# Moving three small products from inside a TensorE group to the boundary one half group earlier

## The chip, the cores and the metric

The kernel runs on one core of one Trainium2 chip. The time is device microseconds of one execution. A core has five engines with queues of their own: TensorE (PE, with its weight loads shown apart as PEld), VectorE (DVE), ScalarE (ACT), GpSimd (POOL) and SyncE (SP). Each takes its instructions in the order in which they are written and waits at a semaphore until another engine or a DMA has counted it up. Everything here is written by hand in that form: one list of instructions for each engine, and named semaphores between them.

## The reference, cut to what matters

Two transformer blocks of width 1024 over 1024 tokens, in fp32. The first ends with a feed-forward layer; the second is scaled and shifted by a vector `mod` that hangs on the input `c` alone:

```
# end of the first block
hid = square(relu(einsum("bsd,df->bsf", h, w_mlp_in)))      # 1024 -> 4096
x   = x + einsum("bsf,fd->bsd", hid, w_mlp_out)             # 4096 -> 1024
# start of the second block
c_act = silu(c)                                             # (1, 1024)
mod   = c_act @ w_ada + b_ada                               # (1, 6144)
sh1, sc1, gt1, sh2, sc2, gt2 = split(mod, 6)
```

`mod` is needed only once the first block is done. The kernel computes it during the first block's feed-forward layer, and that is the place of the change.

## The kernel before, in words

A product of two fp32 matrices is made from three products of high and low parts (hi·hi, lo·hi, hi·lo), all summed in one PSUM bank. A **group** is one 128x512 tile of a result: `group(g, b, ...)` waits on the semaphore `group_free` until bank `b` is empty, issues all matmuls of the tile through `product`, and counts `group_done`.

The feed-forward layer (`ff`) goes through the 4096 hidden columns in eight chunks of 512. Each chunk `i` has on TensorE:
- eight **up groups** n = 0 to 7 of 24 matmuls (8 pieces of the contraction, 3 products each): they fill banks 0 to 3 in turn. ACT takes each result through relu, square and a copy to the high part (lines 864, 866, 870), DVE makes the low part (`hid_lo`, line 1435) and so frees the bank.
- sixteen **down groups** of 12 matmuls (t = 0 to 7, m = 0, 1), which DVE adds to the residual (`xs`, line 1479) and so frees the bank.

Weights come by DMA from SP through four buffers `w_raw`, ACT makes their high part (`w_hi`, line 646) and DVE their low part (`w_lo`, line 1056).

`mod` is made in the six middle chunks (i = 1 to 6) of the first block's layer, 1024 columns of it in each chunk, in four quarters of 256. For one quarter (index n = 0 to 3 of `modulation` on PE) DVE adds up eight **rows**, r = 8n to 8n + 7, into the tile `ada_sum` (line 1452 for the first, line 1454 for the other seven); each row is 128x256 of `w_ada`, weighted by a column of silu(c). Two rows come with one DMA, issued from POOL (line 567), into one of two buffers; POOL issues a DMA when the rows of the one before last are used up. Then PE sums `ada_sum` over the partitions: two matmuls with `one` as the moving operand, of one column each, into bank 4 (line 2048; the profile counts each in two passes, so four). On PE they stand behind a wait for the eight rows. The semaphore `ada_mm` tells DVE that `ada_sum` may be written again, and the first row of the next quarter waits for it.

On DVE the rows stand behind the low parts of the up groups: four behind each of groups 0 to 5, and eight behind group 6. Before the low part of group 0 stand the eight low parts of the weights for the down groups, and behind that of group 7 those for the next up groups, and then the first `xs`. So quarter 0 is complete after the rows behind up group 1, quarter 1 after those behind group 3, quarter 2 after those behind group 5, and quarter 3 after those behind group 6.

On PE the sums of quarters 0, 1 and 2 stand in the middle of up groups 3, 5 and 7, between its twelfth and thirteenth matmul (`between`, lines 1736 and 2062). The sum of quarter 3 stands behind the second down group.

Of the kernel before, what the change touches and what calls it, by code (L numbers as in the profile page):

```python
# [6 lines left out]
def build(nc, a, out):  # L7
# [7 lines left out]
    P = 128  # L15
# [29 lines left out]
    with ctx:  # L45
# [18 lines left out]
        def act_pair(name, o):  # L64
            return (at(name + "_hi", [P, 8, HALF], f32r, o), at(name + "_lo", [P, 8, HALF], f32r, o + SLOT // 2))
# [110 lines left out]
        h2 = [act_pair("h2_0", s2), act_pair("h2_1", s3)]  # L176
# [40 lines left out]
        bank = [ctx.enter_context(nc.psum_tensor(f"bank{i}", [P, 512], f32)) for i in range(8)]  # L217
        XB = bank[4:]

        def sem(name):  # L220
            return ctx.enter_context(nc.semaphore(name))
# [3 lines left out]
        group_done, group_free = sem("group_done"), sem("group_free")  # L225
# [1502 lines left out]
        def _(pe):  # L1728
            mm = nc.tensor.matmul

            def product(out, pairs, between=None):

                n = len(pairs)
                for i, ((lh, ll), (rh, rl)) in enumerate(pairs):
                    if between and i == n // 2:
                        between()
                    mm(out, lh, rh, start=(i == 0), stop=False)  # L1737
                    mm(out, lh, rl, start=False, stop=False)  # L1738
                    last = mm(out, ll, rh, start=False, stop=(i == n - 1))  # L1739
                return last  # L1740

            def group(g, b, width, pairs, rows=P, between=None):
                if not (isinstance(g, int) and g < 4):
                    pe.wait_ge(group_free, g - 3)
                product(bank[b][0:rows, 0:width], pairs, between).then_inc(group_done, 1)

            def chunk_ready(c):
                pe.wait_ge(w_lo, 8 * (c + 1))
# [25 lines left out]
            for j in range(2):  # L1774
                group(j, j, MEM, [((w[0][:, k, j * P:(j + 1) * P], w[1][:, k, j * P:(j + 1) * P]),
                                   (memT[0][:, k, :], memT[1][:, k, :])) for k in range(8)])
            for j in range(2):
                group(2 + j, 2 + j, MEM, [((memT[0][:, k, j * P:(j + 1) * P], memT[1][:, k, j * P:(j + 1) * P]),
                                           (w[0][:, k, 256:512], w[1][:, k, 256:512])) for k in range(8)])
# [5 lines left out]
            def natural(c, par, g, t, width):  # L1785
                group(g, g % 4, width, [(tok(hT, k, t), (W[par][0][:, k, 0:width], W[par][1][:, k, 0:width]))
                                        for k in range(8)])
# [143 lines left out]
            for u, (b, h) in enumerate(ISC):  # L1931
                n = (b + 1) * P
# [14 lines left out]
            with pe.Fori(1, 3) as i:  # L1947
                for j in range(2):
                    par = (C_GATE + j) % 2
                    chunk_ready(2 * i + (C_GATE + j))  # L1950
                    for n in range(8):
                        f, h = n // 2, n % 2
# [72 lines left out]
            for c in range(2):  # L2025
                par = (C_OUT + c) % 2
                chunk_ready(C_OUT + c)
                for t in range(NT):
                    if c == 0 and t % 4 == 0:
                        pe.wait_ge(st_lo, 8 * (t // 4 + 1))  # L2030
                    g = GO + 8 * c + t
                    group(g, g % 4, 512, [(tok(mT, k, t), (W[par][0][:, k, :], W[par][1][:, k, :])) for k in range(8)])

            def norm_transposes(n0, x0, h):
                transposes(n0 + 8 * h, [[xn[:, 4 * h + j, k * P:(k + 1) * P] for j in range(4)] for k in range(8)],
                           lambda n: (n_xn, x0 + 4 * (h + 1)) if n == 0 else None)
                pe.wait_ge(n_lo, n0 + 8 * h + 8)

            def ff(c0, g0, k, n0, x0):


                pa, pb = c0 % 2, 1 - c0 % 2

                def modulation(i, n):

                    pe.wait_ge(ada_s, i * 32 + (8 * n + 8 - 32))
                    for e in range(2):
                        l = mm(bank[4][:, ds(i * 8 + (2 * n + e - 8), 1)], adac[:, e * P:(e + 1) * P], one[:, :],
                               start=True, stop=True)
                    l.then_inc(ada_mm, 1)  # L2050

                def chunk(i, first, last):
                    mod = not (k or first or last)
                    chunk_ready(2 * i + c0)
                    for n in range(8):
                        h, f = n // 4, n % 4
                        if first and n == 4:
                            norm_transposes(n0, x0, 1)
                        group(i * 24 + (g0 + n), n % 4, 512,
                              [((W[pa][0][:, q, f * P:(f + 1) * P], W[pa][1][:, q, f * P:(f + 1) * P]),  # L2060
                                (h2[h][0][:, q, :], h2[h][1][:, q, :])) for q in range(8)],
                              between=(lambda: modulation(i, (n - 3) // 2)) if mod and n in (3, 5, 7) else None)
                    chunk_ready(2 * i + (c0 + 1))
                    for t in range(NT):
                        h, q = t // 4, (t % 4) * P
                        if t % 4 == 0:
                            pe.wait_ge(f_lo, i * 8 + (8 * FC * k + 4 * (h + 1)))
                        for m in range(2):
                            group(i * 24 + (g0 + 8 + 2 * t + m), (2 * t + m) % 4, 512,
                                  [((hid[h][0][:, f, q:q + P], hid[h][1][:, f, q:q + P]),  # L2070
                                    (W[pb][0][:, 2 * f + m, :], W[pb][1][:, 2 * f + m, :])) for f in range(4)])
                            if mod and t == 0 and m == 1:
                                modulation(i, 3)

                norm_transposes(n0, x0, 0)
                if not k:
                    pe.sem_inc(ada_mm, 1)
                chunk(0, True, False)
                with pe.Fori(1, FC - 1) as i:
                    chunk(i, False, False)  # L2080
                chunk(FC - 1, False, True)

            ff(C_FF, GF, 0, 24, 10)
# [27 lines left out]
            for n in range(4):  # L2111
                q = slice((n % 2) * 256, (n % 2) * 256 + 256)
# [38 lines left out]
            for g in range(4):  # L2151
                for par, c in ((0, C_U), (1, C_K)):
                    if g == 0:
                        chunk_ready(c)
                    for h in range(2):
                        n = 2 * par + h
# [102 lines left out]
```

## Time and profile before

| what | us |
|---|---|
| median of 3 runs | 2933.64 |
| lowest and highest of them | 2927.18, 2936.40 |
| the profiled execution, by its own time | 2927.18 |
| its span | 2925.1 |
| the six chunks with `mod` (about) | 1020 to 1560 of the span |

TensorE is busy for 92% of the span, DVE for 48%, ACT for 34% and POOL for 12%. Start times in all rows are microseconds from the start of the span. The six chunks follow each other at 91.4 to 93.5 us, so that what is read in the first stands five more times behind it.

### The profile page before, as it was taken

What the parts mean: (1) busy time and instruction counts of PE and PEld (TensorE: products, weight loads), DVE (VectorE), ACT (ScalarE), POOL (GpSimd) and SP (SyncE); (2) the same over time, 40 slices, a digit from 0 to 9 for tenths busy, and PEclk for the clock granted to TensorE, in tenths of its full rate; (3) what the DMA queues carried; (4) which work ended last, traced back from release to release, by engine and by line L of the source; (5) the groups of instructions that cost most, each with busy time, mean ns of one, the idle gap of its engine ahead of it and who ended that gap; (6) DMA issues with size and microseconds to landing.
All of it is one profiled execution on the core that took longest, in us unless ns stands there. A gap on an engine that the chain in (4) does not pass through costs nothing.

```text
span 2925.1 us, 35932 instructions
## 1 busy us (share of the span) xinstructions
PE 2677.9 (92%) x12620; PEld 2183.2 (75%) x12620; DVE 1417.3 (48%) x3008; ACT 1005.6 (34%) x2052; POOL 339.8 (12%) x524
## 2 busy tenths in 40 slices
PE   5996899988989999999999899977788999999997
PEld 4764788865767788887888677767677888888886
DVE  5266479855543344444543533228444345434345
ACT  6156267545123223221322442236134222223222
POOL 0222512230320011001110000014000000000000
PEclk9999999999999999999999899999799999999998
DMA  4002123331530133222321122131411111011011
GB/s 161 26 30 72 50 76 98 101 129 59 185 122 11 58 116 103 77 90 75 115 90 54 44 84 87 44 101 44 166 36 58 34 53 57 30 56 57 29 43 65
DMA packets 110981, 218.21 MB, mean 75 GB/s; under 512 B 12412, under 2 KB 24324, under 8 KB 110612
## 3 DMA queue, kind: packets, MB, share of 16 engines
q1 hardware_dynamic: 90836, 164.29, 17.2%
q0 software_dynamic: 11968, 37.77, 4.2%
q10 hardware_dynamic: 8064, 14.68, 1.3%
q8 instruction: 66, 1.08, 0.2%
q14 instruction: 47, 0.39, 0.0%
HBM read 183.07 MB, written 33.63 MB: 74 GB/s over the span
## 4 chain that ended last, share of the span: by engine, by line
PE 78%; DVE 9%; ACT 5%; DMA 4%; issue 3%; POOL 1%; SPq 0%; DVEq 0%; ACTq 0%; POOLq 0%
PE bank L1737 23%; PE bank L1739 22%; PE bank L1738 22%; DVE w_lo L1056 1%; ACT w_hi L646 1%; PE bank L1914 1%; PE bank L1915 1%; PE bank L1916 1%; PE bank L1834 1%; DMA w_raw<-in_w_mlp_in 1%; DMA ada<-in_w_ada 1%; DMA w_raw<-in_w_ff 1%; ACT bank L903 1%; ACT h_hi L906 1%; PE bank L1823 1%
## 5 line engine op out<-in xcount | busy, mean ns | idle before, releaser
L1737 PE MATMUL bank<-h_hi,w_hi 128*128 128x512 f32 (+1 forms) x1312 | 516.1, 393 | 19.2 <-DVE h_lo L1522 8.4
L646 ACT ACTIVATE w_hi<-w_raw 128x512 fp32r<-128x512 f32 (+3 forms) x440 | 257.1, 617 | 766.4 <-PE bank L1739 565.0
L1738 PE MATMUL bank<-h_lo,w_hi 128*128 128x512 f32 (+1 forms) x1312 | 511.6, 390 | 0.0
L1739 PE MATMUL bank<-h_hi,w_lo 128*128 128x512 f32 (+1 forms) x1312 | 511.5, 390 | 0.0
L1737 PE MATMUL bank<-w_hi,hid_hi 128*128 128x512 f32 x1024 | 402.2, 393 | 19.5 <-DVEq L1481 19.4
L1739 PE MATMUL bank<-w_hi,hid_lo 128*128 128x512 f32 x1024 | 399.8, 390 | 0.0
L1738 PE MATMUL bank<-w_lo,hid_hi 128*128 128x512 f32 x1024 | 399.5, 390 | 0.0
L1056 DVE TENSOR_TENSOR w_lo<-w_raw,w_hi 128x512 fp32r<-128x512 f32 (+3 forms) x384 | 253.8, 697 | 210.2 <-ACT w_hi L646 203.8
L1737 PEld LDWEIGHTS bank<-h_hi,w_hi 128*128 128x128 f32 x1312 | 249.5, 190 | 73.7 <-DVE h_lo L1522 9.0
L1739 PEld LDWEIGHTS bank<-h_hi,w_lo 128*128 128x128 f32 x1312 | 249.2, 190 | 51.6
L1738 PEld LDWEIGHTS bank<-h_lo,w_hi 128*128 128x128 f32 x1312 | 249.4, 190 | 50.8 <-issue 0.7
L1435 DVE TENSOR_TENSOR hid_lo<-bank,hid_hi 128x512 fp32r<-128x512 f32 x128 | 88.6, 692 | 390.1 <-ACT hid_hi L870 388.6
L1479 DVE TENSOR_TENSOR xs<-xs,bank 128x512 f32<-128x512 f32 x256 | 175.9, 687 | 185.3 <-PE bank L1739 173.8
L1737 PEld LDWEIGHTS bank<-w_hi,hid_hi 128*128 128x128 f32 x1024 | 193.0, 189 | 65.3 <-DVEq L1481 25.8
L1739 PEld LDWEIGHTS bank<-w_hi,hid_lo 128*128 128x128 f32 x1024 | 192.8, 188 | 40.6
L1738 PEld LDWEIGHTS bank<-w_lo,hid_hi 128*128 128x128 f32 x1024 | 193.2, 189 | 39.5
L864 ACT ACTIVATE bank<-bank 128x512 f32<-128x512 f32 x128 | 74.5, 582 | 383.8 <-PE bank L1739 383.8
L567 POOL DMA_DIRECT2D ada<-in_w_ada x96 | 69.5, 724 | 633.4 <-DVE ada_sum L1454 633.2
L1477 DVE TENSOR_TENSOR bank<-bank,rowv 128x512 f32<-128x512 f32 x128 | 89.5, 699 | 104.9 <-PE bank L1739 92.1
L1258 DVE TENSOR_SCALAR_CACHE_REDUCE cmpj<-isc,cand 128x384 bf16<-128x384 f32 (+1 forms) x124 | 100.5, 811 | 7.4 <-DVE cand L1269 5.0
L1454 DVE SCALAR_TENSOR_TENSOR ada_sum<-ada,cact,ada_sum 128x256 f32<-128x256 f32 x168 | 81.5, 485 | 41.4 <-DMA ada<-in_w_ada 34.1
L533 POOL TENSOR_TENSOR w_lo<-w_raw,w_hi 128x512 fp32r<-128x512 f32 x56 | 74.9, 1347 | 227.4 <-ACT w_hi L646 223.0
(401 smaller groups left out, 4138.1 us busy)
## 6 DMA issues: line engine op xcount, KB each, us to landing
w_raw<-in_w_ff SPq DMA_DIRECT2D x128, 256.0 KB, 3.1
w_raw<-in_w_in SPq DMA_DIRECT2D x104, 256.0 KB, 2.7
ada<-in_w_ada POOLq DMA_DIRECT2D x96, 256.0 KB, 3.2
w_raw<-in_w_mlp_in SPq DMA_DIRECT2D x64, 256.0 KB, 3.2
w_raw<-in_w_mlp_out SPq DMA_DIRECT2D x64, 256.0 KB, 3.0
gates_scratch<-gstage ACTq DMA_DIRECT2D x32, 256.0 KB, 2.0
w_raw<-in_w_out SPq DMA_DIRECT2D x32, 256.0 KB, 4.5
stage<-gates_scratch SPq DMA_DIRECT2D x8, 768.0 KB, 5.1
```

The source lines that it names most:

```text
L533: nc.gpsimd.tensor_tensor(W[par][1][:, p, :], raw[:, p % NRAW, :], W[par][0][:, p, :].bitcast(f32), ALU.subtract).then_inc(w_lo, 1)
L646: A_(W[par][0][:, p, 0:n], raw[:, p % NRAW, 0:n], ACT.Copy).then_inc(w_hi, 1)
L864: A_(x, x, ACT.Relu).then_inc(f_r, 1)
L1056: tt(W[par][1][:, p, 0:n], raw[:, p % NRAW, 0:n], W[par][0][:, p, 0:n].bitcast(f32), ALU.subtract).then_inc(w_lo, 1)
L1258: tsc(cmpj[:, 0:(b + 1) * P], isc[b][:, :], cand[:, b - 2:b - 1].bitcast(f32), None, ALU.is_ge, ALU.add, accum_out=cnt[:, b - 2:b - 1]).th ...
L1435: tt(hid[h][1][:, f, :], bank[n % 4][:, :], hid[h][0][:, f, :].bitcast(f32), ALU.subtract)\
L1454: l = stt(adac[:, :], x, cact[:, k:k + 1], adac[:, :], ALU.mult, ALU.add)
L1477: tt(b, b, rowv[:, 512 * m:512 * m + 512], ALU.mult).then_inc(gt_x, 1)
L1479: tt(x, x, bank[(2 * t + m) % 4][:, :], ALU.add).then_inc(x_add, 1)
L1737: mm(out, lh, rh, start=(i == 0), stop=False)
L1738: mm(out, lh, rl, start=False, stop=False)
L1739: last = mm(out, ll, rh, start=False, stop=(i == n - 1))
```

## The change

`product` and `group` lose their parameter `between`. The sums of quarters 0, 1 and 2 now stand behind up groups 2, 4 and 6, that is ahead of all 24 matmuls of groups 3, 5 and 7 instead of behind the first twelve. Quarter 3 stays where it is. The other engines' instructions are the same and in the same order.

```
-            def product(out, pairs, between=None):
+            def product(out, pairs):
 
                 n = len(pairs)
                 for i, ((lh, ll), (rh, rl)) in enumerate(pairs):
-                    if between and i == n // 2:
-                        between()
                     mm(out, lh, rh, start=(i == 0), stop=False)
...
                         group(i * 24 + (g0 + n), n % 4, 512,
                               [((W[pa][0][:, q, f * P:(f + 1) * P], W[pa][1][:, q, f * P:(f + 1) * P]),
-                                (h2[h][0][:, q, :], h2[h][1][:, q, :])) for q in range(8)],
-                              between=(lambda: modulation(i, (n - 3) // 2)) if mod and n in (3, 5, 7) else None)
+                                (h2[h][0][:, q, :], h2[h][1][:, q, :])) for q in range(8)])
+                        if mod and n in (2, 4, 6):
+                            modulation(i, (n - 2) // 2)
```

Here is TensorE's queue at the sum of quarter 0 before the change, in the middle of up group 3. `ada_sum` is DVE's sum of the rows, `h_0` the layer's input, and the row in which the wait stands is the weight load of the sum.

```order
L1737 MATMUL bank<-h_0_hi,w_hi 128x512
L1738 MATMUL bank<-h_0_lo,w_hi 128x512
L1739 MATMUL bank<-h_0_hi,w_lo 128x512
L2046 ISA
L2048 ISA [waits ada_sum]
L2048 MATMUL bank<-one,ada_sum 128x1
L2048 ISA
L2048 MATMUL bank<-one,ada_sum 128x1
L1737 MATMUL bank<-h_0_hi,w_hi 128x512
L1738 MATMUL bank<-h_0_lo,w_hi 128x512
```

And here is the same queue after it, at the boundary of up groups 2 and 3 (its line numbers are two lower).

```order
L1735 MATMUL bank<-h_0_hi,w_hi 128x512
L1736 MATMUL bank<-h_0_lo,w_hi 128x512
L1737 MATMUL bank<-h_0_hi,w_lo 128x512
L2044 ISA
L2046 ISA [waits ada_sum]
L2046 MATMUL bank<-one,ada_sum 128x1
L2046 ISA
L2046 MATMUL bank<-one,ada_sum 128x1
L1742 REGISTER_ALU
L1735 MATMUL bank<-h_0_hi,w_hi 128x512 [waits group_free]
```

The wait for the rows has moved ahead of the twelve matmuls that stood between the start of group 3 and the sum, and with it stands ahead of the whole of group 3. Quarters 1 and 2 move in the same way.

## Rows read from the trace of the kernel before

**Rows 1.** The page: busy us of each engine, share of the span, instructions.

```profile
PE 2677.9 (92%) x12620; PEld 2183.2 (75%) x12620; DVE 1417.3 (48%) x3008; ACT 1005.6 (34%) x2052; POOL 339.8 (12%) x524
```

**Rows 2.** Who waited for whom, 1020 to 1560: total us, times, longest.

```profile
PE bank L1737 <- DVEq L1481: 13.3, 6, 2.7
```

**Rows 3.** Timeline, PE, first chunk, group 3: start, us, instruction, [idle before <-releaser].

```profile
1037.52 0.39 PE L1737 MATMUL bank<-h_hi,w_hi 128*128 128x512 f32 x1
...
1040.01 0.64 PEld L2048 LDWEIGHTS bank<-one,ada_sum 128*128 128x128 f32 x4
1040.24 0.50 PE L2048 MATMUL bank<-one,ada_sum 128*128 128x1 f32 x4
...
1040.60 0.48 PE L1737 MATMUL bank<-h_hi,w_hi 128*128 128x512 f32 x1
```

**Rows 4.** Timeline, ACT's relu: ends of groups 2, 3, 4; group 2, chunks 3, 4.

```profile
1037.72 0.58 ACT L864 ACTIVATE bank<-bank 128x512 f32<-128x512 f32 x1 [3.61 <-PE bank L1739]
...
1043.65 0.58 ACT L864 ACTIVATE bank<-bank 128x512 f32<-128x512 f32 x1 [4.11 <-PE bank L1739]
...
1049.09 0.58 ACT L864 ACTIVATE bank<-bank 128x512 f32<-128x512 f32 x1 [3.61 <-PE bank L1739]
...
1222.20 0.58 ACT L864 ACTIVATE bank<-bank 128x512 f32<-128x512 f32 x1 [3.61 <-PE bank L1739]
...
1313.65 0.58 ACT L864 ACTIVATE bank<-bank 128x512 f32<-128x512 f32 x1 [3.61 <-PE bank L1739]
```

**Rows 5.** Timeline, DVE: last rows of quarter 0, chunks 1, 3, 4.

```profile
1038.22 1.00 DVE L1454 SCALAR_TENSOR_TENSOR ada_sum<-ada,cact,ada_sum 128x256 f32<-128x256 f32 x2 [0.39 <-DMA ada<-in_w_ada]
...
1222.89 1.01 DVE L1454 SCALAR_TENSOR_TENSOR ada_sum<-ada,cact,ada_sum 128x256 f32<-128x256 f32 x2 [0.58 <-DMA ada<-in_w_ada]
...
1313.89 1.01 DVE L1454 SCALAR_TENSOR_TENSOR ada_sum<-ada,cact,ada_sum 128x256 f32<-128x256 f32 x2 [0.39 <-DMA ada<-in_w_ada]
```

**Rows 6.** Timeline: quarters 1 and 2, last rows on DVE and sums on PE.

```profile
1057.79 2.05 DVE L1454 SCALAR_TENSOR_TENSOR ada_sum<-ada,cact,ada_sum 128x256 f32<-128x256 f32 x4 [0.21 <-DVE hid_lo L1435]
...
1062.99 0.50 PE L2048 MATMUL bank<-one,ada_sum 128*128 128x1 f32 x4
...
1139.09 1.01 DVE L1454 SCALAR_TENSOR_TENSOR ada_sum<-ada,cact,ada_sum 128x256 f32<-128x256 f32 x2 [0.23 <-DMA ada<-in_w_ada]
...
1143.04 0.50 PE L2048 MATMUL bank<-one,ada_sum 128*128 128x1 f32 x4
```

**Rows 7.** The chain of waits, second chunk: start, us, what.

```profile
1154.57 0.35 PE bank L2048 x4
...
1155.03 0.36 DVE ada_sum L1452
...
1157.25 3.53 DMA ada<-in_w_ada
...
1162.00 0.70 DVE hid_lo L1435
...
1165.00 3.54 DMA w_raw<-in_w_mlp_in
```

**Rows 8.** Timeline, DVE behind low parts 0 and 6; PE's release, first chunk.

```profile
1032.45 0.35 DVE L1452 TENSOR_SCALAR ada_sum<-ada,cact 128x256 f32<-128x256 f32 x1 [0.33 <-DVE hid_lo L1435]
...
1062.32 0.69 DVE L1435 TENSOR_TENSOR hid_lo<-bank,hid_hi 128x512 fp32r<-128x512 f32 x1 [2.49 <-ACT hid_hi L870]
1063.60 0.36 DVE L1452 TENSOR_SCALAR ada_sum<-ada,cact 128x256 f32<-128x256 f32 x1 [0.59 <-DMA ada<-in_w_ada]
...
1079.06 0.68 DVE L1479 TENSOR_TENSOR xs<-xs,bank 128x512 f32<-128x512 f32 x1
...
1079.85 0.50 PE L1737 MATMUL bank<-w_hi,hid_hi 128*128 128x512 f32 x1 [2.12 <-DVEq L1481]
```

**Rows 9.** Stretches of 1 us: busy us (x) by engine, granted clock, DMA share, GB/s.

```profile
1172.00:1173.00 1.00, 1.00 (x4) 0.81 (x3) 0.70 (x2) 0.00 (x0) 0.00 (x0) 0.50 0.79 262
...
1357.00:1358.00 1.00, 1.00 (x4) 0.81 (x3) 0.70 (x2) 0.00 (x0) 0.00 (x0) 0.50 0.72 240
```

More of the change, by code:

```diff
@@ L1740, in product, with group @@
                 return last
-            def group(g, b, width, pairs, rows=P, between=None):
+            def group(g, b, width, pairs, rows=P):
                 if not (isinstance(g, int) and g < 4):
                     pe.wait_ge(group_free, g - 3)
-                product(bank[b][0:rows, 0:width], pairs, between).then_inc(group_done, 1)
+                product(bank[b][0:rows, 0:width], pairs).then_inc(group_done, 1)
             def chunk_ready(c):
```

## The prediction, made before the changed kernel was run

> **What bounds the kernel now.** I read the page first: TensorE is busy for 92% of the span [rows 1], so a microsecond that PE stands still is lost unless it stood still later anyway. Then the table of who waited for whom over the six chunks that make `mod`: PE waits there for one thing only, DVE's `xs` additions, six times, 13.3 us in all [rows 2]. That is one stall of about 2.1 us in each chunk, ahead of the fifth down group, where the first bank that `xs` must free is wanted again [rows 8]. PE never waited for `ada_sum`. The chain of waits tells what sets the end of that stall. It leaves PE at the sum of quarter 2, goes over to DVE (the first row of quarter 3), through a transfer of `ada`, the low part of group 7 and a transfer of `w_raw`, and comes back at the first `xs` [rows 7, 8]. So in each chunk the end is set by PE up to about group 7, then by DVE, and from the fifth down group on by PE again. What matters for the change is when `ada_sum` is full and where PE stands then, which the timeline gives.
>
> **The change: the sums themselves.** No instruction is added or removed on any engine; 18 sums (three in each of six chunks) stand twelve matmuls earlier. A sum takes 0.36 us of PE ahead of the next product, and that product's own row is 0.48 instead of 0.39 us long [rows 3]. A group with a sum in it ends 5.93 us after the one before (1037.72 to 1043.65 by ACT's relu), one without it 5.44 us (to 1049.09) [rows 4]: 0.5 us for each sum in the middle of a group. I take the same at a boundary, thus nothing. The bounds are a gain of 18 x 0.5 = 9 us, if it were free there, and a loss of as much if it cost double. Neither has a row for it: the step between matmuls is the same across the end of a group as within it (24 x 0.227 = 5.44), so a boundary has no gap to hide a sum in.
>
> **Quarter 0, where a wait appears.** Group 3's first matmul starts at 1037.52 and the sum twelve matmuls later at 1040.24 [rows 3], that is 2.72 us. The last of the eight rows ends at 1038.22 + 1.00 = 1039.22 [rows 5]. Where the sum stands now, there is about 1 us to spare; where it will stand, PE arrives at 1037.52, 1.70 us too early. The rows end that late because DVE waits for `ada` (the row names the DMA), behind the low parts of the weights and of groups 0 and 1. The same in the others: ACT's relu starts 0.20 us after PE's next group (1037.72 against 1037.52 [rows 3, 4]), so in the third chunk PE would arrive at 1222.00 and the rows end at 1223.90, 1.90 us; in the fourth at 1313.45 and 1314.90, 1.45 us [rows 4, 5]. These are the largest and the least of six; the mean of the six is 1.71 us.
>
> To this comes the way from DVE to PE. From the end of an `xs` (1079.06 + 0.68) to PE's restart are 0.11 us [rows 8]. The weight load of a sum normally runs 0.23 us ahead of it, under the last matmul (1040.01 against 1040.24 [rows 3]); after a wait this lead may be lost. That bounds the addition by 0.11 and 0.11 + 0.23 = 0.34 us. I take 0.2, nearer to the first, since the restart in rows 8 shows no gap of its own ahead of the matmul. One stall is then 1.71 + 0.2 = 1.91 us, six are 11.5 us. Behind the waiting load stand all 24 matmuls of group 3 and everything later on PE; ACT waits for them, and the DVE's low part of group 3 for ACT. What the six could be at least is 0 (below, absorption), at most 6 x (1.90 + 0.34) = 13.4 us.
>
> **Quarters 1 and 2.** Their rows follow a low part with little wait, and all this moves with PE. For quarter 2 the rows end at 1057.79 + 2.05 = 1059.84 and PE would arrive at 1062.99 - 2.72 = 1060.27; with the load's lead of 0.23 and the way of 0.11 there are 0.09 us left [rows 6]. Quarter 1 in the second chunk is the tightest of the twelve: 1140.10 against 1143.04 - 2.72 = 1140.32, where the load would be 0.12 us late. But that row waited 0.23 us for its `ada` transfer [rows 6], and PE's delay at quarter 0 moves the low part of group 3 back and not this transfer. I cost both at nothing. Bounds: nothing, and 0.3 us for each of the six quarters 1 (1.8 us); a stall at quarter 2 falls into the time that PE loses at the fifth down group anyway.
>
> **What comes back.** The first row of quarter 3 starts 1.28 us after the low part of group 6 (1062.32 to 1063.60 [rows 8]). The page names the transfer there, but in the next chunk's chain it is released by PE's sum of quarter 2 (1154.57 + 0.35 = 1154.92, row starts 1155.03 [rows 7]). With that sum ahead of group 7 the row can follow the low part as directly as the one behind group 0: 0.69 us of work and 0.33 idle, 1.02 us [rows 8]. The gain is 0.26 us on DVE, and since the chain runs through exactly this row, the first `xs` comes 0.26 us less late than PE does. PE's stall of 2.12 us shrinks by that: six times 0.25 is 1.5 us. At least it is 0, if the transfer decides; at most the stall, the absorption below.
>
> **The clock.** After two of the six stalls of about 2.1 us the granted clock fell to 0.50, the 1.2 GHz level [rows 9]: behind those of the second and the fourth chunk. What one fall costs: relu to relu, two chunks with one fall take 1222.20 - 1037.72 = 184.48 us, the next, without one, 91.45 [rows 4]; 184.48 - 2 x 91.45 = 1.58 us. The changed kernel stands still twice in a chunk, twelve times instead of six. At two in six, the six new stalls would bring two falls; the old stalls get a little shorter, which may save one. I add one fall, 1.6 us; the bounds are -3.2 (both of now gone) and +9.5 (all six new ones).
>
> On this the Trainium skill, page "TensorE: Matmul & The Clock Gate", section "HAM oscillation — how this bites in real kernels", speaks against the change: a product stream broken by a wait in every round can be throttled again in every round. The trace agrees in part, with two in six [rows 9]. What the rule would make of the time is the second rival.
>
> **The sum.** 11.5 (quarter 0) + 0 (quarters 1, 2) + 0 (the sums) - 1.5 (row of quarter 3) + 1.6 (clock) = 11.6 us. Against the profiled span of 2925.1 us that gives 2936.7 us, in its own time of 2927.18 us 2938.8 us. That execution was the lowest of three, 6.5 us below the median; on the median of 2933.64 us it is 2945 us, 0.4% slower.
>
> **Rivals.**
> *Absorption (not slower).* The stall at the fifth down group swallows the delay: the first `xs` keeps its time, PE merely comes later to a wait that it had anyway. 13.3 us of waiting [rows 2] against 11.5 us is enough for it. It decides from the point where the DVE's work behind group 6 hangs on a transfer that doesn't move with PE, as the row names it in the first chunk [rows 8]. Against it: these `ada` transfers are issued only when DVE has used the rows before, and `w_raw` only when `w_lo` is made, so both move with DVE, which itself waits 2.49 us for ACT and PE at low part 6 [rows 8]. It would give 0 to -1.5 us, about 2933 us on the median.
> *The clock falls each time.* Every one of the six new stalls ends at half clock: 10.0 + 6 x 1.58 = 19.5 us, 2953 us. For it: each stall is as long as those that already did it. Against it: four of six did not.
> *The margin at quarters 1 and 2 is gone too.* 0.09 us is little. With 0.2 us lost at each quarter 1: 1.2 us more, 2946 us.
>
> **How the numbers follow.** Chances: the forecast 0.60, the clock each time 0.14, the margin gone 0.08, absorption 0.18. What a measurement of this kernel can tell from no change is about 0.3%, 8.8 us. The forecast's own range is 7 to 16 us more, 2940 to 2949 us; a part of it (0.18 of its 0.60) is below 8.8 us, and runs of one kernel lie 9 us apart. Slower: 0.42 + 0.14 + 0.06 = 0.62. Same: 0.18 + 0.02 + 0.12 of absorption = 0.32. Faster: 0.06, the rest of absorption. The range with 8 in 10: 2935 us (most of absorption left out) to 2954 us (the clock's case in).
>
> **What would show it.** Right: PE waits for `ada_sum` (line 2046 there) six times, 1.6 to 2.2 us each and 11 to 12 in total, ahead of group 3 alone; the wait for `xs` is still there six times and about 1.8 us long; chunks are 93 us apart without a fall of the clock (91.45 + 1.65); the first row of quarter 3 starts about 1.0 us after low part 6; three falls of the clock in the six chunks. Wrong: no wait at line 2046, or a wait for `xs` that shrank by as much as the new one is long (then absorption), or 18 waits, or a distance of groups with a sum other than 5.93 us.

## The result

The changed kernel takes 2950.24 us (median of 6 runs, 2944.15 to 2952.92) against 2933.40 us (median of 6, 2927.18 to 2936.40). The ratio is 1.0054, with a 95% interval of 1.0040 to 1.0069: slower by 0.54% (11.7 to 20.2 us by the interval; the medians lie 16.8 us apart). The forecast was 11.6 us more (2945 us), with a range of 2935 to 2954 us. The profiled execution took 2945.62 us, its span 2943.5 us.

### The profile page after: what moved, and what is told of

Same layout as the page of the kernel before. It is cut to its first block, busy times and chain, and to the rows that moved or that the text cites. A ratio compares the mean times of both kernels' runs of the same rounds, so it can differ in the third digit from the quotient of the medians.

```text
span 2943.5 us, 35932 instructions
## 1 busy us (share of the span) xinstructions
PE 2687.8 (91%) x12620; PEld 2187.8 (74%) x12620; DVE 1417.9 (48%) x3008; ACT 1005.4 (34%) x2052; POOL 338.6 (12%) x524
## 4 chain that ended last, share of the span: by engine, by line
PE 74%; DVE 10%; ACT 6%; DMA 5%; issue 3%; POOL 1%; SPq 0%; DVEq 0%; ACTq 0%; POOLq 0%
PE bank L1735 21%; PE bank L1736 21%; PE bank L1737 21%; DVE w_lo L1056 2%; DMA ada<-in_w_ada 2%; DVE ada_sum L1454 1%; ACT w_hi L646 1%; PE bank L1912 1%; PE bank L1913 1%; PE bank L1914 1%; PE bank L1832 1%; DMA w_raw<-in_w_ff 1%; DMA w_raw<-in_w_mlp_in 1%; ACT bank L903 1%; DMA w_raw<-in_w_mlp_out 1%
```

## The profile after

PE's busy time grew by 9.9 us [rows 1] while the span grew by 18.4, so its share fell from 92% to 91%:

```profile
PE 2687.8 (91%) x12620; PEld 2187.8 (74%) x12620; DVE 1417.9 (48%) x3008; ACT 1005.4 (34%) x2052; POOL 338.6 (12%) x524
```

Who PE waited for in the six chunks (1020 to 1580 here): total us, times, longest.

```profile
PE bank L1735 <- DVEq L1481: 13.0, 6, 2.9
PE bank L2046 <- DVE ada_sum L1454: 10.1, 6, 1.9
```

The first line answers to the only one of before [rows 2] and is as large as it was; the second is new: six waits for `ada_sum`, one in each chunk, though three sums in each were moved. In the timeline of the first chunk DVE, PE and ACT look like this (start, us, instruction, [idle before <-releaser]):

```profile
1037.27 1.00 DVE L1454 SCALAR_TENSOR_TENSOR ada_sum<-ada,cact,ada_sum 128x256 f32<-128x256 f32 x2 [1.64 <-DMA ada<-in_w_ada]
1038.39 0.58 ACT L864 ACTIVATE bank<-bank 128x512 f32<-128x512 f32 x1 [3.61 <-PE bank L1737]
...
1038.61 1.01 DVE L1454 SCALAR_TENSOR_TENSOR ada_sum<-ada,cact,ada_sum 128x256 f32<-128x256 f32 x2 [0.34 <-DMA ada<-in_w_ada]
1039.77 0.52 PEld L2046 LDWEIGHTS bank<-one,ada_sum 128*128 128x128 f32 x4 [1.84 <-issue]
1039.78 0.60 PE L2046 MATMUL bank<-one,ada_sum 128*128 128x1 f32 x4 [1.43 <-DVE ada_sum L1454]
...
1040.24 0.49 PE L1735 MATMUL bank<-h_hi,w_hi 128*128 128x512 f32 x1
...
1046.02 0.58 ACT L864 ACTIVATE bank<-bank 128x512 f32<-128x512 f32 x1 [5.81 <-PE bank L1737]
```

PE was through group 2 at about 1038.19, 0.20 us ahead of ACT's relu. The last row of quarter 0 ends at 1038.61 + 1.01 = 1039.62, the weight load of the sum starts 0.15 us later. Group 3 ends by ACT's relu 7.63 us after group 2, where it was 5.93 us [rows 4]. The idle time in the row (1.43 us) is less than what was lost (1.70 us). PE's record holds the end of the last matmul of group 2 as busy (about 0.16 us), and from the start of the sum to the next product it is 0.46 us instead of 0.36 [rows 3]. So the step from relu to relu is the better measure. In the 16 chunks of three profiles of the changed kernel in which the clock didn't fall in group 3, the step is 7.40 to 8.09 us, 7.81 in the mean, 1.88 us more than before.

The sums of quarters 1 and 2 found their rows: no wait, and an ordinary step of 5.93 us:

```profile
1051.27 0.50 PE L2046 MATMUL bank<-one,ada_sum 128*128 128x1 f32 x4
...
1062.64 0.50 PE L2046 MATMUL bank<-one,ada_sum 128*128 128x1 f32 x4
```

The granted clock fell four times in the six chunks, where the kernel before had two [rows 9]. Two of the falls stand behind new waits (in the third and sixth chunk), two behind the wait for `xs`. Stretches of 1 us, the first and third behind `xs`, the other two behind the sum of quarter 0; columns as in rows 9:

```profile
1085.00:1086.00 1.00, 1.00 (x4) 0.81 (x3) 0.69 (x1) 0.00 (x0) 0.00 (x0) 0.50 0.08 29
...
1231.00:1232.00 1.00, 1.00 (x4) 0.77 (x3) 0.60 (x2) 0.00 (x0) 0.00 (x0) 0.50 0.65 209
...
1368.00:1369.00 1.00, 1.00 (x4) 0.80 (x3) 0.70 (x2) 0.00 (x0) 0.00 (x0) 0.50 0.60 211
...
1515.00:1516.00 1.00, 1.00 (x4) 0.72 (x3) 0.25 (x2) 0.00 (x0) 0.69 (x1) 0.50 0.02 8
```

## The experiments

The kernel before ran on the same chip in each set: median 2934.85 us (19 runs) in the first, 2934.71 us (25 runs, without one of 7665.52 us) in the second. Each edit is against the kernel before unless the text says otherwise. The theory: the whole loss is PE's wait for the rows of quarter 0, which DVE's later chain neither absorbs nor enlarges, plus the falls of the clock behind it. The rivals: the new place costs by itself, or with quarters 1 and 2; absorption; a wait costs by breaking something, not by its length.

### Quarter 0 alone

```
-  between=(lambda: modulation(i, (n - 3) // 2)) if mod and n in (3, 5, 7) else None)
+  between=(lambda: modulation(i, (n - 3) // 2)) if mod and n in (5, 7) else None)
+                        if mod and n in (2,):
+                            modulation(i, (n - 2) // 2)
```

> The kernel before with the sum of quarter 0 alone moved to the boundary behind up group 2; quarters 1 and 2 stay in the middle of groups 5 and 7. My theory (the whole loss is PE's wait for the rows of quarter 0, passed on to the end): six waits of 1.4 to 1.9 us ahead of group 3, 10 us in total, and 12 to 17 us more than before, as much as all three moved. Rival (each of the three moved sums costs its share, by standing at a boundary or by a margin lost): 5 us more, a third.

Measured: 2952.61 us, ratio 1.0065 (1.0048 to 1.0082). PE's waits in the six chunks:

```profile
PE bank L1737 <- DVEq L1481: 14.8, 6, 2.7
PE bank L2048 <- DVE ada_sum L1454: 10.5, 6, 2.0
```

17.8 us more, a little above what I had expected, and nothing like a third of the loss. This profile had five falls of the clock, one behind a new wait and four behind `xs`. One moved sum of three carries the whole loss.

### Quarters 1 and 2 alone

```
-  between=(lambda: modulation(i, (n - 3) // 2)) if mod and n in (3, 5, 7) else None)
+  between=(lambda: modulation(i, (n - 3) // 2)) if mod and n in (3,) else None)
+                        if mod and n in (4, 6):
+                            modulation(i, (n - 2) // 2)
```

> The kernel before with the sums of quarters 1 and 2 moved to the boundaries behind up groups 4 and 6, quarter 0 left in the middle of group 3. My theory: no wait for the rows on PE, the first row of quarter 3 comes up to 0.26 us sooner, 0 to 1.5 us less than before. Rival (boundaries or lost margins cost): 8 to 11 us more.

Measured: 2937.98 us, ratio 1.0004 (0.9991 to 1.0016). The median is 3.1 us higher where I had expected 0 to 1.5 us less, but the interval (2.6 us less to 4.7 more) holds both. No loss of 8 us, so the rival is out; the small gain is not shown. In four chunks the sum of quarter 1 found its rows. In the second and third the step of the groups was 6.13 and 6.17 us instead of 5.93, and the rows that were late are those with a transfer behind them. DVE, then PE, in the second chunk:

```profile
1146.64 1.01 DVE L1454 SCALAR_TENSOR_TENSOR ada_sum<-ada,cact,ada_sum 128x256 f32<-128x256 f32 x2 [0.23 <-DVE hid_lo L1435]
1148.08 1.01 DVE L1454 SCALAR_TENSOR_TENSOR ada_sum<-ada,cact,ada_sum 128x256 f32<-128x256 f32 x2 [0.43 <-DMA ada<-in_w_ada]
```

```profile
1149.22 0.60 PE L2048 MATMUL bank<-one,ada_sum 128*128 128x1 f32 x4
```

The sum starts 0.13 us behind the end of the rows, and its record is 0.60 us long, as behind a real wait, though no idle time shows. In the changed kernel, where quarter 0 holds PE up by 1.88 us, no chunk has this. That is what the prediction said of its tightest place: the transfer's time goes into the delay.

### The boundary without a wait

```
-  between=(lambda: modulation(i, (n - 3) // 2)) if mod and n in (3, 5, 7) else None)
+  between=(lambda: modulation(i, (n - 3) // 2)) if mod and n in (5, 7) else None)
+                        if mod and n in (3,):
+                            modulation(i, (n - 3) // 2)
```

> The kernel before with the sum of quarter 0 moved the other way, from the middle of group 3 to the boundary behind it; quarters 1 and 2 unchanged. It measures the boundary without a wait. My theory: a sum costs 0.5 us there as in the middle, no wait on PE, time as before within 2 us; DVE's row 8 waits some 2.4 us longer, off the path. Rival (a sum at a boundary costs more than in the middle, since the next group's wait for its bank stands behind it): 6 x 0.3 us or more, seen as a step of 6.2 us or more from group 3 to group 4.

Measured: 2935.39 us, ratio 1.0000 (0.9991 to 1.0010). ACT's relu for groups 2, 3 and 4 of the second chunk, with the sum between the last two:

```profile
1130.60 0.58 ACT L864 ACTIVATE bank<-bank 128x512 f32<-128x512 f32 x1 [3.62 <-PE bank L1739]
1136.04 0.58 ACT L864 ACTIVATE bank<-bank 128x512 f32<-128x512 f32 x1 [3.62 <-PE bank L1739]
1141.97 0.58 ACT L864 ACTIVATE bank<-bank 128x512 f32<-128x512 f32 x1 [4.11 <-PE bank L1739]
```

5.44 and 5.93 us: a sum at a boundary costs 0.49 us, as in the middle. The place itself is free of charge and of gain.

### Quarter 2 later: what the first `xs` hangs on

```
-  between=(lambda: modulation(i, (n - 3) // 2)) if mod and n in (3, 5, 7) else None)
+  between=(lambda: modulation(i, (n - 3) // 2)) if mod and n in (3, 5) else None)
+                        if mod and n in (7,):
+                            modulation(i, (n - 3) // 2)
```

> The kernel before with the sum of quarter 2 moved from the middle of group 7 to the boundary behind it. My theory (the first xs hangs on this sum through the first row of quarter 3): that row comes 2.7 us later, PE's wait ahead of the fifth down group grows from 2.2 to about 4.9 us, 16 us more than before and more falls of the clock, 2950 us or more. Rival (that wait is set by weight transfers that keep their time, which is also what absorption would need): no change.

Measured: 2954.35 us, ratio 1.0067 (1.0050 to 1.0084), 19.5 us more. DVE, and PE behind it, in the first chunk:

```profile
1065.25 0.69 DVE L1435 TENSOR_TENSOR hid_lo<-bank,hid_hi 128x512 fp32r<-128x512 f32 x1 [2.49 <-ACT hid_hi L870]
1069.25 0.35 DVE L1452 TENSOR_SCALAR ada_sum<-ada,cact 128x256 f32<-128x256 f32 x1 [3.31 <-PE bank L2048]
...
1085.17 0.68 DVE L1479 TENSOR_TENSOR xs<-xs,bank 128x512 f32<-128x512 f32 x1
```

```profile
1076.32 0.60 PE L2048 MATMUL bank<-one,ada_sum 128*128 128x1 f32 x4 [1.59 <-DVE ada_sum L1454]
1085.96 0.79 PE L1737 MATMUL bank<-w_hi,hid_hi 128*128 128x512 f32 x1 [3.44 <-DVEq L1481]
```

The first row of quarter 3 starts 4.00 us behind low part 6, where it was 1.28 us [rows 8]: 2.72 us later, as expected, and from there to the first `xs` 15.9 us, where it was 15.5. So the chain is real and moves with this sum. One thing I had wrong: PE's extra time isn't one wait of 4.9 us; 1.6 us of it are spent already at the sum of quarter 3, which now comes too early, and 3.4 us ahead of the fifth down group. The clock fell in all six chunks.

### A shorter wait

```
-                    if between and i == n // 2:
+                    if between and i == at:
...
-  between=(lambda: modulation(i, (n - 3) // 2)) if mod and n in (3, 5, 7) else None)
+  between=(lambda: modulation(i, (n - 3) // 2)) if mod and n in (3, 5, 7) else None, at=2 if n == 3 else 4)
```

> The kernel before with the sum of quarter 0 behind six of group 3's 24 matmuls instead of twelve; all else as before. PE comes there 1.36 us later than at the boundary. If the loss is the waiting time alone, each chunk loses what is left of the wait: 1.9 - 1.36 = 0.5 us, 3 us in all, with no more falls of the clock than before: 2936 to 2939 us. If a wait costs mainly by what it breaks (a fall of the clock, the lead of the weight load), whatever its length, it loses more than half of what the full move lost: 8 us or more.

Measured: 2938.88 us, ratio 1.0015 (1.0005 to 1.0025): 4.2 us. The profile has six waits for `ada_sum`, 2.9 us in all, the longest 0.5, and one fall of the clock, behind `xs`. By relu to relu group 3 takes 6.58 to 6.75 us, 0.74 us more in the mean than an ordinary step with a sum; with quarter 0 alone at the boundary it was 2.0 us more in the five chunks without a fall in group 3. The loss goes down with the length of the wait.

### Rows early: the wait taken away

The changed kernel, with rows 0 to 3 ahead of the low parts of the weights (so that the next two transfers of `ada` run beside these) and rows 4 to 7 behind low part 0:

```
+                    if mod:
+                        for r in range(4):
+                            modulation(i, r)
                     split_lo(2 * i + (c0 + 1), 1 - c0 % 2)
...
-                        if mod and n < 7:
-                            for r in range(4 * n, 4 * n + 4 if n < 6 else 32):
+                        if mod and n < 7 and n != 1:
+                            for r in range(4 * max(n, 1), 4 * max(n, 1) + 4 if n < 6 else 32):
```

> The changed kernel, with the first four rows of each chunk put ahead of the low parts of the down groups' weights and rows 4 to 7 behind low part 0, so that quarter 0 is full before PE reaches the boundary behind group 2. Same instructions, another order on DVE. My theory (the loss is the wait for these rows, and they are late by the transfers of ada): no wait for the rows ahead of group 3, no falls of the clock there, time as before or up to 1.5 us less: 2931 to 2936 us. Rival (the new place costs by itself): still 10 us or more over before.

Measured: 2935.56 us, ratio 1.0005 (0.9994 to 1.0016). DVE at quarter 0 in the second chunk, and PE's waits in the six chunks:

```profile
1135.24 0.69 DVE L1435 TENSOR_TENSOR hid_lo<-bank,hid_hi 128x512 fp32r<-128x512 f32 x1 [1.12 <-ACT hid_hi L870]
1136.16 2.05 DVE L1454 SCALAR_TENSOR_TENSOR ada_sum<-ada,cact,ada_sum 128x256 f32<-128x256 f32 x4 [0.23 <-DVE hid_lo L1435]
```

```profile
PE bank L1738 <- DVEq L1484: 12.6, 6, 3.2
PE bank L2049 <- DVE ada_sum L1454: 0.4, 2, 0.2
```

Rows 4 to 7 run without a gap for `ada`, the waits of 10.1 us shrink to 0.4, and with them the loss goes to within the interval (1.8 us less to 4.7 more), at the same order on PE. A small rest is left: group 3 takes 6.09 to 6.40 us by relu to relu, 0.3 us more in the mean than the ordinary 5.93, some 2 us in all. In the second chunk the rows end at 1136.16 + 2.05 = 1138.21, where PE is through group 2 at about 1138.08. The two falls of the clock are both behind the wait for `xs`.

### Rows 28 to 31 late, in both kernels

```
-                            for r in range(4 * n, 4 * n + 4 if n < 6 else 32):
+                            for r in range(4 * n, 4 * n + 4):
...
+                        if mod and t in (3, 4):
+                            for r in range(28 + 2 * (t - 3), 30 + 2 * (t - 3)):
+                                modulation(i, r)
...
-                            if mod and t == 0 and m == 1:
+                            if mod and t == 5 and m == 1:
```

In the kernel before:

> The kernel before with rows 28 to 31 taken from behind low part 6 and put behind the xs additions of t = 3 and 4, and the sum of quarter 3 behind the down group t = 5, m = 1. It takes the two transfers of ada and four rows out of DVE's way to the first xs. If the wait ahead of the fifth down group hangs on them, the first xs comes about 2.2 us sooner, the wait goes to under 0.4 us in each chunk, the falls of the clock go with it: 13 us of waiting and two falls (3 us) less, 2917 to 2921 us. If the weight transfers set it anyway: less than 4 us gained.

Measured: 2920.01 us (2919.24 to 2922.14), ratio 0.9956 (0.9941 to 0.9971). This version beats both kernels. PE's waits in the six chunks:

```profile
PE bank L1740 <- DVEq L1481: 1.3, 4, 0.5
```

Of 13.3 us [rows 2] 1.3 are left, and the clock doesn't fall in any of the six chunks. Twelve microseconds of waiting and two falls make the 14.7 us.

In the changed kernel:

> The changed kernel with the same late rows 28 to 31. It asks whether the wait for quarter 0 and the wait for the first xs are independent. My theory: both parts add. The six waits ahead of group 3 stay at 1.4 to 1.9 us, those for xs go: 16 us less than the changed kernel and 12 to 17 us more than the kernel before with late rows, so near the kernel before, 2930 to 2936 us. Rival (the wait for xs had absorbed a part of the delay): more over the kernel before with late rows than 17 us.

Measured: 2936.28 us, ratio to the kernel before 1.0004 (0.9992 to 1.0016); 16.3 us more than the kernel before with the same late rows. PE's waits:

```profile
PE bank L2049 <- DVE ada_sum L1454: 11.6, 6, 2.1
PE bank L1738 <- DVEq L1481: 2.1, 6, 0.5
```

With the wait for `xs` nearly gone, the change costs 16.3 us, and with it 16.8 us, each known to within some 4 us. That the two agree so closely is in part luck. In chunks without a fall the change costs 2.2 us here (89.6 to 91.8 us from chunk to chunk) and 1.6 us with the wait for `xs`. About half of the difference is that the new waits are longer here (a step of 8.13 us in the mean of five, against 7.81); the other half is the 0.3 us that came back in each chunk and doesn't here. So of a delay of nearly 2 us the wait for `xs` gave back no more than this.

### The falls of the clock, counted again

Unchanged copies of both kernels, two profiles each.

> The changed kernel once more, for its falls of the clock in the six chunks (its first profile had four, two behind the new waits; the kernel before two). If a fall behind a wait of about 2 us is a matter of chance that stands between the two kernels, the count differs from profile to profile, 3 to 6 here, with falls behind both kinds of wait. If the changed kernel has no more falls than before: 1 to 3, and the excess over the forecast is elsewhere.

> As the first look at the changed kernel: 3 to 6 falls if they come by chance behind twelve waits, 1 to 3 if the new waits bring none.

> The kernel before once more: 1 to 3 falls of the clock in the six chunks, all behind the wait ahead of the fifth down group, if they come by chance behind six waits.

> As the first look at the kernel before: 1 to 3 falls, all behind the wait ahead of the fifth down group.

Measured: the changed kernel had three falls each time, all behind the wait for `xs` (2946.58 and 2941.55 us); the kernel before two each time, behind `xs` as well (2929.71 and 2929.65 us). With the first profiles the means are 3.3 and 2.0. The count is within both expectations at its edge; that every changed profile has falls behind new waits isn't so.

## Why the prediction was right, point by point

The mechanism came out as forecast, term by term. The size was short: 16.8 us between the medians against 11.6, which lies just below the measured interval (11.7 to 20.2), and outside the 7 to 16 us that the prediction gave its own case. The total is nearer to the 19.5 us of the second rival, whose mechanism did not happen. The wide range held it because it had been drawn to take that rival in.

**Quarter 0** was sized at 1.91 us a chunk, from 1.71 us of missing rows and 0.2 us of way. 1.88 us is measured, in 16 chunks. Moving only this sum gives the whole loss, making its rows early takes it away, and shortening the wait by 1.36 us leaves 4.2 us of it: shown.

**Quarters 1 and 2** were costed at nothing: shown in the changed kernel by ordinary steps of 5.93 us in all three profiles, and by the experiment that moves them alone, to within its interval. The margin that I had called small is indeed gone in two of six chunks when quarter 0 doesn't move along, at 0.2 us each.

**The sums** cost the same at a boundary: shown, 5.93 us a step both ways.

**What comes back** was set at 0.25 us a chunk. From the relu of group 3 to that of the next chunk's group 2, in chunks without a fall, the kernel before takes 85.63 us (mean of 12, three profiles) and the changed one 85.31 us (mean of 10). That is 0.32 us back. These chunks are 93.1 us apart, as forecast. The chain under it is shown by the sum of quarter 2 moved later.

The row itself starts 1.00 us behind low part 6 in four of the six chunks, as in DVE's timeline of the second, where it was 1.28 us [rows 8]:

```profile
1160.52 0.69 DVE L1435 TENSOR_TENSOR hid_lo<-bank,hid_hi 128x512 fp32r<-128x512 f32 x1 [2.48 <-ACT hid_hi L870]
1161.52 0.36 DVE L1452 TENSOR_SCALAR ada_sum<-ada,cact 128x256 f32<-128x256 f32 x1 [0.30 <-DVE hid_lo L1435]
```

In the first and the fourth chunk it waits for its transfer instead, in each of the three profiles, and nothing comes back: 1.56 to 1.78 us behind low part 6 in the first, where it was 1.28, and 1.54 to 1.56 in the fourth, where it was 1.50 to 1.59 before. That was the prediction's lower bound ("if the transfer decides"), and the row of the first chunk in rows 8 named the transfer. GpSimd issues this transfer late there. DVE's rows whose first two free the buffer start at 1060.16 and 1156.00 us in the first and second chunk, the issues 2.49 and 1.31 us later:

```profile
1062.65 1.45 POOL L567 DMA_DIRECT2D ada<-in_w_ada  x2 [5.31 <-DVE ada_sum L1454]
...
1157.31 0.72 POOL L567 DMA_DIRECT2D ada<-in_w_ada  x1 [4.21 <-DVE ada_sum L1454]
```

Why the issue comes late in these two chunks, before the change as well, isn't shown.

**The clock** was the least certain term: one fall more, 1.6 us. Measured are 1.3 more on three profiles each, about 2 us. Where the clock falls is uneven, as the last section tells.

**The sum over the six chunks**, relu of group 2 in the first to the same in the chunk behind the sixth: 552.36, 553.03 and 552.65 us before, 566.96, 564.76 and 564.76 us after, in the mean 12.8 us more against 11.6 forecast. The terms as measured make 6 x (1.88 - 0.32) + 2 = 11.4 us. The rest of it, about 1.4 us, lies in the chunks with a fall: they take 93.2 us in the mean of six before and 95.1 in the mean of ten after, 1.9 us more, where those without a fall take 1.6 more. Six of the ten are the first and the fourth chunk, in which the first row of quarter 3 waits for its transfer:

```profile
1066.48 0.35 DVE L1452 TENSOR_SCALAR ada_sum<-ada,cact 128x256 f32<-128x256 f32 x1 [1.09 <-DMA ada<-in_w_ada]
```

**What stays open.** The medians lie 16.8 us apart, 4 us more than the six chunks of the profiles. Outside the six chunks the spans of the profiles are 2372.7, 2374.6 and 2375.0 us before and 2376.5, 2379.7 and 2374.8 us after. That is 3 us more in the mean, at a scatter of up to 5 us within one kernel, in stages in which no instruction moved. It goes with the clock: read in stretches of 1 us outside the chunks (0 to 1035 and 1600 to 2900), the granted clock was at 0.50 for 178, 184 and 184 us before and 195, 205 and 181 after, in nearly the same order as the spans. Ahead of 1035 us, where all kernels are the same, it was 68 to 85 us from profile to profile. So I don't call the 3 us an effect of the change.

**The rivals.** Absorption is out: the wait for `xs` was 13.7 us in the mean of three profiles before and 12.8 after, 2.3 and 2.1 us each (the prediction had 1.8 after), and with it nearly gone the change still costs 16.3 us. It fell where the prediction said it would decide: the transfers behind group 6 are issued when DVE is done with the rows before, and so move with PE. The clock falling each time is out: it fell behind two of 18 new waits. The margin at quarters 1 and 2 was not needed.

## What to carry to other kernels

Small work that waits for another engine should stand in the queue where its data are ready, not where a boundary is tidy: what counts is everything behind it in that queue, here 24 matmuls held up for a sum of 0.5 us. An idle time further on doesn't forgive the delay by its size alone; follow the chain of waits back from its end, and if it starts at work that the delay moves, it moves too. The same chain shows what is worth changing: four rows and two transfers taken out of it gave 14.7 us, where moving the sums gave back 0.3 us a chunk.

## What the runs showed of the hardware

A wait of PE of about 2 us is followed by a fall to 1.2 GHz only sometimes, and the two kinds of wait differ. Behind the waits ahead of group 3 (1.2 to 2.1 us) it fell 4 times in 30, behind those ahead of the fifth down group (1.7 to 3.0 us, counted in the kernels whose DVE order is that of before, without the one that moves quarter 2) 25 times in 60. These 25 are not spread evenly: 9 of 10 in the fourth chunk and 7 of 10 in the first, against 9 of 40 in the other four. The length of the wait alone doesn't decide it: in the kernel before the clock fell behind 2.12 us in the second chunk and stayed up behind 2.12 us in the first. What does isn't shown. Behind waits of 0.4 to 0.6 us ahead of group 3 it did not fall in six cases. Where PE waited twice in a chunk, 1.5 to 1.7 us at the sum of quarter 3 and up to 3.4 us some 9 us later, it fell in six of six, five times behind the second wait and once behind the first. Where no wait in the six chunks is longer than 0.55 us and the clock stays up, the runs also lay closer together, 2919.24 to 2922.14 us in 5 runs against 2927.18 to 2936.40 in 6 of the kernel before. So a part of this kernel's scatter may be these falls; that was not counted run by run.
